# An expert loop that fetches the next item's token rows by an indirect DMA from row numbers, in place of selection products

## What is computed

```python
def moe_swiglu(h, w_router, b_router, w1, w3, w2):
    logits = (h @ w_router).astype(jnp.float32) + b_router.astype(jnp.float32)
    top_val, top_idx = lax.top_k(logits, TOP_K)
    top_w = jax.nn.softmax(top_val, axis=-1)
    gate = jnp.einsum('blk,blke->ble', top_w,
                      jax.nn.one_hot(top_idx, N_EXPERTS, dtype=jnp.float32)).astype(h.dtype)
    out = jnp.zeros_like(h)
    for e in range(N_EXPERTS):
        out = out + gate[..., e:e + 1] * swiglu(h, w1[e], w3[e], w2[e])
    return out
```

## Time and profile before

| | |
|---|---|
| median of 3 runs | 2504.99 us (2501.67 to 2508.28) |
| span of the profiled execution | 2504.6 us |
| expert loop, 8 items | from about 1493 us to the end |
| one item | 124.4 us |

### The profile page before, as it was taken

How to read it: one execution, slowest core, us unless ns; L and a number is a source line. 1 busy time by engine, 2 the same in 40 slices (tenths; PEclk the granted TensorE clock), 3 DMA queues, 4 the chain that set the end, 5 groups by cost and what they waited for, 6 DMA issues and landing times.

```text
span 2504.6 us, 35552 instructions
## 1 busy us (share of the span) xinstructions
PE 2462.0 (98%) x12958; PEld 2078.3 (83%) x12958; DVE 1910.0 (76%) x2267; ACT 1458.6 (58%) x1741; POOL 91.6 (4%) x141
## 2 busy tenths in 40 slices
PE   8999999999999999999999999999999999999997
PEld 8787889999987788888788878888888888888886
DVE  6667876455578777456798469999999999998998
ACT  4445343444444353443544447877878777878786
POOL 0000000000010000010110000000000000000000
PEclk9999999999999999998999989999999999999999
DMA  7456766665568763453798349999999999999995
GB/s 249 162 188 219 261 230 192 179 146 155 154 152 270 251 215 93 111 56 47 278 372 310 118 168 356 348 362 347 363 347 362 349 360 349 359 350 360 347 360 217
DMA packets 289124, 633.34 MB, mean 253 GB/s; under 512 B 10842, under 2 KB 72309, under 8 KB 288704
## 3 DMA queue, kind: packets, MB, share of 16 engines
q1 hardware_dynamic: 268512, 556.83, 63.2%
q0 software_dynamic: 20512, 75.11, 12.1%
HBM read 630.75 MB, written 1.14 MB: 252 GB/s over the span
## 4 chain that ended last, share of the span: by engine, by line
PE 93%; DVE 5%; ACT 1%; issue 1%; DMA 1%; DVEq 0%; SPq 0%; ACTq 0%
PE ps L716 28%; PE ps L718 27%; PE ps L717 27%; PE ps L863 1%; DVE w_lo L2173 1%; ACT w_hi L1612 1%; PE ps L1353 1%; PE ps L1095 1%; PE ps L1110 1%; PE ps L740 1%; PE ps L1390 1%; PE ps L1115 1%; PE ps L1387 1%; PE ps L1374 1%; PE ps L1341 1%
## 5 line engine op out<-in xcount | busy, mean ns | idle before, releaser
L2173 DVE TENSOR_TENSOR w_lo<-raw,w_hi 128x1024 fp32r<-128x1024 f32 x722 | 873.6, 1224 | 466.0 <-ACT w_hi L1612 443.3
L1612 ACT ACTIVATE w_hi<-raw 128x1024 fp32r<-128x1024 f32 x722 | 755.7, 1059 | 673.7 <-PE ps L718 659.3
L716 PE MATMUL ps<-w_hi,x_hi 128*128 128x512 f32 (+1 forms) x1936 | 744.0, 384 | 5.9 <-DVE x_lo L2190 4.0
L718 PE MATMUL ps<-w_hi,x_lo 128*128 128x512 f32 (+1 forms) x1936 | 727.3, 376 | 0.0
L717 PE MATMUL ps<-w_lo,x_hi 128*128 128x512 f32 (+1 forms) x1936 | 726.3, 375 | 0.0
L716 PEld LDWEIGHTS ps<-w_hi,x_hi 128*128 128x128 f32 x1936 | 366.3, 189 | 89.4 <-issue 16.9
L718 PEld LDWEIGHTS ps<-w_hi,x_lo 128*128 128x128 f32 x1936 | 366.1, 189 | 67.3
L2173 DVE TENSOR_TENSOR w_lo<-big,w_hi 128x1024 fp32r<-128x1024 f32 x336 | 404.3, 1222 | 19.8 <-ACT w_hi L1612 0.2
L717 PEld LDWEIGHTS ps<-w_lo,x_hi 128*128 128x128 f32 x1936 | 366.8, 189 | 61.9 <-issue 1.0
L1612 ACT ACTIVATE w_hi<-big 128x1024 fp32r<-128x1024 f32 x336 | 358.1, 1066 | 94.1 <-PE ps L718 94.0
L716 PE MATMUL ps<-w_hi,h_hi 128*128 128x512 f32 x760 | 297.2, 391 | 1.2
(11 more groups left out here) (405 smaller groups left out, 2206.6 us busy)
## 6 DMA issues: line engine op xcount, KB each, us to landing
raw<-in_moe_w SPq DMA_DIRECT2D x170, 1024.0 KB, 5.2
big<-in_moe_w SPq DMA_DIRECT2D x168, 1024.0 KB, 5.3
big<-in_w_ada POOLq DMA_DIRECT2D x48, 1024.0 KB, 7.6
raw<-in_ffn_w_up SPq DMA_DIRECT2D x44, 1024.0 KB, 5.2
raw<-in_attn_w_in SPq DMA_DIRECT2D x36, 1024.0 KB, 5.0
raw<-in_ffn_w SPq DMA_DIRECT2D x33, 1024.0 KB, 7.7
raw<-in_ret_w_in SPq DMA_DIRECT2D x24, 1024.0 KB, 5.2
raw<-in_ffn_w_down SPq DMA_DIRECT2D x22, 1024.0 KB, 5.3
```

The costliest lines, as they stand in the source:

```text
L716: mm(dst, lhs[0], rhs[0], start=start, stop=False)
L718: return mm(dst, lhs[1], rhs[0], start=False, stop=stop)
L1612: nc.scalar.activation(w_hi[:, m % SPLIT, :], raw(SLOT_OF[b])[:, h * HALF:(h + 1) * HALF], ACT.Copy).then_inc(hi_ready, 1)
L2173: V.tensor_tensor(w_lo[:, m % SPLIT, :], raw(SLOT_OF[b])[:, h * HALF:(h + 1) * HALF], w_hi[:, m % SPLIT, :].bitcast(F32), ALU.subtract).th ...
```

## The change

The token rows are written once to a buffer in memory, `x_rows`. In each item PE finds only the row number of each slot, and GpSimd fetches the rows.

- **Once, in the Fourier stage:** VectorE makes `tok_ids`, the number of each token twice, from the diagonal of identity times the iota tile: seven small operations.
- **Once, at the start of the expert stage:** GpSimd waits until both token parts are saved, adds them (`m_both`, 128x2048), writes 1 MB to `x_rows` and waits for it. It then reads `count` and enters a loop of its own.
- **In each item, PE:** `next_high` (8 products of 512 columns) becomes `next_index`, two products of `m_sel` by `tok_ids` with 2 columns. `next_low` becomes `next_turned`: the same 8 transposes, one block later (after block 6), and they wait for `rows_in` instead of ACT's copy. They read `m_g[:, 0]`, where the rows land (`m_rows` is the same place).
- **In each item, VectorE:** `weights()` begins with a wait for the index products and one operation on 128x1 that turns them into the integer `row_at`, no larger than 255.
- **In each item, GpSimd:** it waits for `row_at`, multiplies two 128x1 columns (`turn_mark`), and issues the indirect DMA, 128 rows of 4 KB.
- **In each item, ACT:** `keep(0)` is gone. `keep(1)`, now the only one, stands one block later.

Slots without a token now hold row 0 (or row 255 where the sum is larger) instead of zeros; their gate is zero.

```diff
+        x_rows_dram = nc.dram_tensor("x_rows", [T, D], F32, kind="Internal").ap()
...
@@ GpSimd
+            nc.gpsimd.memset(turn_mark[:, 0:1], 0.0).then_inc(marked, 1)
+            pool.wait_ge(m_tok_saved, 8)
+            nc.gpsimd.tensor_tensor(m_both, m_tok_hi[:, :, :].bitcast(F32), m_tok_lo[:, :, :].bitcast(F32), ALU.add
+                                    ).then_inc(rows_added, 1)
+            pool.wait_ge(rows_added, 1)
+            pool.dma_start(x_rows_dram.rearrange("(t p) d -> p t d", p=P), m_both).then_inc(rows_kept, 16)
+            pool.wait_ge(rows_kept, 16)
+            pool.wait_ge(table_ready, 1)
+            count = pool.value_load(table[0:1, ITEMS - 1:ITEMS], min_val=EXPERTS, max_val=ITEMS - 1)
+            with pool.Fori(0, count) as e:
+                pool.wait_ge(row_kept, e + 1)
+                pool.wait_ge(marked, e + 1)
+                nc.gpsimd.tensor_tensor(turn_mark[:, 1:2], turn_mark[:, 0:1], turn_mark[:, 0:1], ALU.mult
+                                        ).then_inc(marked, 1)
+                nc.gpsimd.indirect_dma_start(m_rows, None, x_rows_dram, bass.IndirectOffsetOnAxis(row_at[:, 0:1], 0)
+                                             ).then_inc(rows_in, 16)
...
@@ PE
-                def next_high():
+                def next_index():
...
-                    for half in range(2):
-                        c = slice(half * BANK, half * BANK + BANK)
-                        for t in range(TT):
-                            mm(ps[:, half, :], m_sel[:, t, :], m_tok_hi[:, t, c], start=t == 0, stop=False)
-                            last = mm(ps[:, half, :], m_sel[:, t, :], m_tok_lo[:, t, c], start=False, stop=t == TT - 1)
-                    last.then_inc(gathered, 1)
+                    for t in range(TT):
+                        last = mm(ps[:, 0, 0:2], m_sel[:, t, :], tok_ids[:, t, :], start=t == 0, stop=t == TT - 1)
+                    last.then_inc(row_found, 1)
-                def next_low():
-                    pe.wait_ge(m_g_saved, e * 2 + 3)
-                    for k in range(KD):
-                        last = nc.tensor.transpose(psf[:, k * P:(k + 1) * P], m_g[:, 0, k, :], ident)
-                    last.then_inc(gathered, 1)
+                def next_turned(n):
+                    if n == 6:
+                        pe.wait_ge(rows_in, e * 16 + 16)
+                        for k in range(KD):
+                            last = nc.tensor.transpose(psf[:, k * P:(k + 1) * P], m_g[:, 0, k, :], ident)
+                        last.then_inc(gathered, 1)
...
@@ VectorE, weights()
+                    dve.wait_ge(row_found, e + 1)
+                    V.tensor_scalar(row_at[:, :], ps[:, 0, 0:1], float(T - 1), None, ALU.min).then_inc(row_kept, 1)
                     dve.wait_ge(m_x_cut, e + 1)
                     select_weighted(e)
```

## The result

The changed kernel takes 2543.02 us (median of 4 runs, 2539.23 to 2548.16) against 2506.64 us for the kernel before, measured beside it. The ratio is 1.015, with a 95% interval of 1.0133 to 1.0167: slower by 36 us. I had forecast 2497, with 8 chances in 10 between 2492 and 2513. The span of the profiled execution is 2542.6 us.

What follows compares the result with a forecast made beforehand. PE's instruction stream was taken to bound the loop. 8 x (1.45 - 0.3) = 9.2 us gained, 1.5 lost at the start: 2504.99 - 7.7 = 2497.3 us, with 8 chances in 10 between 2492 and 2513.

Steps and rivals of the forecast that it cites:

- The bound: Expert loop: goes by PE's instruction stream, PE busy 124.36 of 124.50 us in an item; loads are paced by compute.
- What leaves PE: Each item: 8 selection products (1.83 us) replaced by 2 index products (0.38 us), a gain of 1.45 us.
- When PE asks: Each item: PE reaches its wait for the rows, after block 6, 9.20 us after the end of block 3.
- the 8 transposes stay: Each item on PE: the transposes remain, as long as they were, so moving them was given no cost.
- When GpSimd can start: Each item: `row_at` is ready 3.4 us after block 3, behind block 5's cuts, leaving 5.8 us for GpSimd and transfer.
- What GpSimd and the transfer take: Each item: 5.3 plain load, 0.2 mark, 0.6 indirect addressing, 6.1 us against 5.8 available; PE waits 0.3 us.
- that rival: GpSimd and VectorE block each other in the loop: up to 1.2 us lost per item, about 2508 us; chance 0.17.
- PE's clock: PE's clock should not fall behind a wait: after 2.16 us of idle the granted clock was still 1.00.
- The start: Start of expert stage: GpSimd's sum may hold VectorE's routing chain; 1.5 us lost once, from 0.6 to 3 us.
- Memory: Rival: 355 GB/s is the ceiling, an item takes 1.1 us more, 2515 us in all; chance 0.05.
- The late gather: Rival: full DMA engines delay the rows, PE waits 3.3 us in each item, 2521 us; chance 0.15.

Runs made afterwards that it cites:

- no_wait_early: Changed kernel with the 8 transposes between blocks 5 and 6, reading a tile always there, PE waiting for gathered rows only at the item's end: 2496.67 us.
- early_low: Changed kernel with GpSimd's sum later, row numbers found earlier, and `h_lo` made between the two halves of block 6's cut: 2491.19 us.
- held: Changed kernel with one wait more: VectorE cuts block 6 only after GpSimd has issued the gather: 2515.68 us.
- late_sum: Changed kernel with GpSimd's sum of the token parts waiting until VectorE has cut `x_lo` of the first item: 2537.55 us.
- alone: Changed kernel with one gather more, of row 0, ahead of the loop while VectorE is idle, sum and write after it: one run, 2546 us.

## Why the prediction was wrong

**The bound** was right. Where nothing waits for the rows, an item is shorter by what PE is spared (no_wait_early, early_low), and SP still waits for VectorE's buffers.

**What leaves PE** was right in kind and a little small: 1.60 us in place of 1.45, because the two index products cost 0.23 us and not twice a weight load of 0.19. With the `h_lo` wait out of the way, the items come out 1.6 us shorter (no_wait_early, 122.6 against 124.2).

**When PE asks.** I had 9.20 us after block 3; it was 9.69 (1635.48 to 1645.17). The step that failed here is "the 8 transposes stay": moved past the wait for `h_lo`, they uncovered it. While the rows are late this shifts PE's question and costs nothing of its own; once they are in time it costs 0.9 us in each item.

**When GpSimd can start** was about right: the gather starts 0.6 us after `row_at`, where I had put 0.2 for the mark and a little for the semaphores: 3.8 us after block 3, against 3.6 in my sum.

**What GpSimd and the transfer take** was the failed step, and it decided the sign: 5.9 us from the start of the issue to landing became 9.3, and the wait of 0.3 us became 3.8 + 9.3 - 9.7 = 3.4. The plain load in this loop takes 6.3 us, 1.0 more than the 5.3 that I chose between the rows with lighter traffic. The indirect form takes 0.4 us more on GpSimd than the plain one when it is free (0.97 against 0.57), within my 0 to 1. VectorE's two cuts take 2.2 us. These make 8.9; the last 0.4 us lie behind the issue and stay open.

The cuts stood in my sum with nothing. I had named that rival, gave it 0.17, and priced it at 1.2 us with "there is over a microsecond of gap". The price and the gap were both wrong. In the earlier trace rows VectorE idles 0.72 us before its next cut at 1634.21, because it waits for ACT's `w_hi`. ACT's rounding, before and after, the start and what it waited for:

```profile
1633.12 1.06 ACT L1612 ACTIVATE w_hi<-raw 128x1024 fp32r<-128x1024 f32 x1 [2.14 <-PE ps L718]
```

```profile
1637.27 1.06 ACT L1638 ACTIVATE w_hi<-raw 128x1024 fp32r<-128x1024 f32 x1 [0.53 <-PE ps L746]
```

That is 3.41 us after the first selection product and 1.79 us after the first index product: 1.6 us earlier, as much as PE is spared. So the idle time was made by the very products that the change removes: they kept PE from block 4, PE kept ACT from `w_hi`, and ACT kept VectorE. With the products gone, the cut follows `row_at` by half a microsecond, its fellow follows without a gap, and GpSimd stands behind both. The gather began 0.03 us too late to come first, and the mark ahead of it had taken 0.37 us; whether a gather without the mark gets in ahead of the cuts was not run.

The page "SBUF — State Buffer" of the Trainium skill, section "Who interferes with whom", states such a lock between a VectorE instruction with two SBUF inputs and a GpSimd instruction that reads SBUF. The runs agree with it: in the mark (0.22 to 2.24 us, early_low), in the gather (0.97 to 3.17 us, held against the changed kernel), and in VectorE's own operation (0.16 to 4.27 us, late_sum against the changed kernel).

**PE's clock.** I said that it would not fall, from one idle stretch of 2.16 us. The waits here were longer than that, and it fell behind most of them, for 1.8 us in each item on average. A row on a shorter stretch doesn't speak for a longer one.

**The start.** I took 1.5 us out of 0.6 to 3. It was 2.8 us: the sum took 4.57 us, near twice the 2.5 at VectorE's rate, and the chain stood still from its third small operation on. Some 0.6 us more went with the low clock in the first blocks (12.98 us from PE's first block to its index products, against 12.42).

**The account.** For one item: 1.6 gained; 0.9 for `h_lo`, 3.4 for the rows and 1.8 for the clock lost: 4.5, as measured (128.7 - 124.2). In the spans: 3.2 us up to the first index products, 31.6 over the seven distances, and 3.2 from the last index products to the end make 38.0, against 36 in the medians. With the wait of 3.4 us alone my sum would have given about 2522; the rest is mostly the clock and `h_lo`, which I had put at nothing.

**The other rivals.** Memory was no bound: in early_low an item moves 363 GB/s at full speed of PE. The late gather was priced with a wait of 3.3 us, and it is chance that this is near the measured 3.4, of which 2.2 are the cuts. That the engines' load makes the gather late was true for 1 us, against the load that I took, and for 2.5 us against the free gather of alone (4.5 to 7.0 us, both with about 1 us on GpSimd).

## What to carry to other kernels

Before work is taken from the engine that bounds a kernel, look whether the gaps on the other engines, in which new work is to fit, hang on that work: they go with it. A GpSimd instruction that reads SBUF, an indirect DMA's issue included, may have to wait for a whole run of VectorE's two-input operations (here two, 2.2 us), and the reverse; place it where VectorE is idle, or give it the time of that run. And a wait of several microseconds on TensorE can cost more than itself, because the clock may fall (here 3.4 us and 1.8 more); ask for such data late, or find its address early.

## What the runs showed of the hardware that I had not expected

- Issuing an indirect DMA took 0.97 us of GpSimd, with 128 rows of 4 KB. With two VectorE cuts across it, it took 3.17 us, and with 64 rows 3.12.
- It landed 4.5 us after the start of its issue with DMA engines otherwise idle, 6.4 to 7.0 beside the stream of weights, 9.3 behind two cuts. Repeated rows cost nothing.
- VectorE's cuts, issued back to back, let a waiting GpSimd instruction in only behind the last of the two, except in one item of early_low, where it came in between them; in the other direction a GpSimd sum of 128x2048 held VectorE for 4.3 us.
- Behind PE's wait the clock stayed at 1.00 in the first and the last item (3.02 and 3.62 us) and fell in the six others (3.02 to 3.77 us). In late_sum it fell behind 2.69 us and stayed behind 2.77. So the length of the wait alone doesn't decide it; what else does stays open. No run was made on it.
